# Expert weights split in place in ten to twelve homes, with the down chunks two blocks behind

## The reference

```python
def swiglu(h, w1, w3, w2):
    return (jax.nn.silu(h @ w1) * (h @ w3)) @ w2

def moe_swiglu(h, w_router, w1, w3, w2):
    logits = (h @ w_router).astype(jnp.float32)
    top_val, top_idx = lax.top_k(logits, TOP_K)
    top_w = jax.nn.softmax(top_val, axis=-1)
    combine = jnp.sum(jax.nn.one_hot(top_idx, N_EXPERTS, dtype=jnp.float32) * top_w[..., None], axis=-2)
    out = jnp.zeros_like(h)
    for e in range(N_EXPERTS):
        out = out + combine[..., e:e + 1].astype(h.dtype) * swiglu(h, w1[e], w3[e], w2[e])
    return out
```

## Time and profile before

| | |
|---|---|
| median of 3 runs | 1847.54 us (1846.96 to 1848.07) |
| the profiled execution, its own time | 1846.31 us |
| its span | 1844.6 us |
| TensorE clock granted in it, share of full | 0.998 |
| PE busy | 1795.8 us, 97% of the span |
| DVE busy | 1526.0 us, 83% |
| ACT busy | 1236.8 us, 67% |
| moved by DMA | 519.91 MB, mean 282 GB/s |

### The profile page before, as it was taken

The page is one execution under the profiler, slowest core; times in us unless marked ns, Lnnn a source line. Parts: engine busy times, 40 slices in busy tenths (PEclk is TensorE's granted clock), DMA queues, the critical chain, the costliest instruction groups (busy, mean ns, idle before and its releaser), DMA issues.

```text
span 1844.6 us, 25231 instructions
## 1 busy us (share of the span) xinstructions
PE 1795.8 (97%) x10094; PEld 1523.3 (83%) x10094; DVE 1526.0 (83%) x1402; ACT 1236.8 (67%) x1144; POOL 76.7 (4%) x97
## 2 busy tenths in 40 slices
PE   9999999999999999999999999999999999999997
PEld 9989998999999989998988766787677876778765
DVE  7999866575558999965598899888998899988997
ACT  5656745554445566744576788778887788877886
POOL 1000000100001000000200000000001000010000
PEclk9999999999999999999999999999999999999999
DMA  8544554445445544545399999999999999999994
GB/s 335 182 163 158 183 183 160 155 178 193 182 159 180 195 160 160 183 183 183 139 388 390 343 408 421 393 376 370 418 421 397 374 366 422 421 396 370 373 421 190
DMA packets 75845, 519.91 MB, mean 282 GB/s; under 512 B 9360, under 2 KB 9616, under 8 KB 14544
## 3 DMA queue, kind: packets, MB, share of 16 engines
q1 hardware_dynamic: 72464, 507.84, 71.3%
q0 software_dynamic: 2544, 9.18, 1.7%
q10 hardware_dynamic: 720, 1.31, 0.2%
HBM read 511.74 MB, written 6.55 MB: 281 GB/s over the span
## 4 chain that ended last, share of the span: by engine, by line
PE 74%; DVE 16%; ACT 6%; issue 3%; DMA 1%; SPq 0%; ACTq 0%; DVEq 0%
PE psum L1946 15%; PE psum L1932 13%; PE psum L1934 13%; PE psum L1933 13%; DVE wlo L1205 13%; PE psum L1947 7%; ACT whi L665 5%; PE psum L2434 3%; PE psum L2435 2%; PE psum L2453 1%; DVE U L1789 1%; PE psum L2200 1%; PE psum L2180 1%; DMA raw<-in_stream 1%; PE psum L2416 1%
## 5 line engine op out<-in xcount | busy, mean ns | idle before, releaser
L1205 DVE TENSOR_TENSOR wlo<-raw,whi 128x2048 fp32r<-128x2048 f32 x369 | 837.3, 2281 | 194.0 <-ACT whi L665 192.8
L665 ACT ACTIVATE whi<-raw 128x2048 fp32r<-128x2048 f32 x369 | 700.0, 1904 | 144.9 <-PE psum L1934 82.2
L1946 PE MATMUL psum<-h_hl,whi 128*128 128x512 f32 x1216 | 430.1, 398 | 0.3 <-DVE U L1563 0.2
L1947 PE MATMUL psum<-h_hl,wlo 128*128 128x256 f32 x1216 | 340.3, 280 | 0.0
L1932 PE MATMUL psum<-whi,act_hl 128*128 128x512 f32 x736 | 293.3, 399 | 7.9 <-DVE wlo L1205 6.4
L1934 PE MATMUL psum<-whi,act_hl 128*128 128x512 f32 x736 | 287.7, 391 | 0.0
L1933 PE MATMUL psum<-wlo,act_hl 128*128 128x512 f32 x736 | 287.3, 390 | 0.0
L1946 PEld LDWEIGHTS psum<-h_hl,whi 128*128 128x128 f32 x1216 | 228.2, 188 | 55.0 <-issue 1.2
L1947 PEld LDWEIGHTS psum<-h_hl,wlo 128*128 128x128 f32 x1216 | 229.5, 189 | 0.1
L1932 PE MATMUL psum<-act_hl,whi 128*128 128x256 f32 x720 | 206.3, 287 | 1.4 <-DVE wlo L1205 0.7
L2434 PE MATMUL psum<-whi,h_hl 128*128 128x512 f32 x448 | 183.7, 410 | 21.0 <-DVE wlo L1205 20.3
(11 more groups left out here) (295 smaller groups left out, 2231.7 us busy)
## 6 DMA issues: line engine op xcount, KB each, us to landing
raw<-in_stream SPq DMA_DIRECT2D x366, 1024.0 KB, 6.7
U<-in_stream SPq DMA_DIRECT2D x74, 1024.0 KB, 8.2
memhat<-in_stream SPq DMA_DIRECT2D x37, 1024.0 KB, 8.0
raw<-in_stream SPq DMA_DIRECT2D x6, 512.0 KB, 3.8
xacc<-U POOLq DMA_DIRECT2D x3, 512.0 KB, 7.6
xT<-in_x_cols ACTq DMA_DIRECT2D x4, 256.0 KB, 6.5
raw<-in_stream SPq DMA_DIRECT2D x4, 256.0 KB, 7.2
memhat<-in_mem_cols SPq DMA_DIRECT2D x1, 1024.0 KB, 19.7
```

The source lines that it names most:

```text
L665: act.activation(whi[:, n % SPLIT, 0:words], src[:, 0:words], ACT.Copy).then_inc(hi_ready, 1)
L1205: dve.tensor_tensor(wlo[:, n % SPLIT, 0:words], src[:, 0:words], whi[:, n % SPLIT, 0:words].bitcast(F32), ALU.subtract).then_inc(lo_ready, 1)
L1946: pe.matmul(o[:].rearrange("p (a b) -> p a b", a=2), st[0], mv, start=start, stop=False)
L1947: return pe.matmul(o[:, 0:256], st[1], mv[:, 0, :], start=False, stop=stop)
```

## The change

In the expert part the low part is written into the home itself, over the raw words, so that `wlo` isn't used there; a home is free only when PE has used the chunk. There are ten homes (a part of `h_hl` is the tenth) until chunk 46 (`JOINED`), and twelve from there on (`xT` and another piece of `U`). The high homes stay three. The down chunks of step s stand behind the ups of step s + 2 (they stood behind those of s + 1). In a few step the turn stands behind the ups (before: between gates and ups), and the fold behind the downs (before: between ups and downs). The gathered tokens of the next expert are transposed by halves in steps f = 4 and 5, through bank 7, behind the ups; only expert 0 still does all of it in step 6. `halves_kept`, `rows_out` and the routing's small work move by one or two chunks.

```diff
-EXTRAS = 3
+EXTRAS, LATER = 4, 2
 RING = RAW + EXTRAS
+DEPTH = SPLIT
+JOINED = 46
...
 def gate_end(s):
-    return 6 * s - 1 if s else 1
+    return 6 * s - 3 if s > 1 else 4 * s + 1
...
 def down_end(s):
-    return up_end(s + 1) + 2 if s < STEPS - 1 else TOTAL - 1
+    return min(up_end(s + 2) + 2, TOTAL - 1 - 2 * (STEPS - 1 - s))
...
+def due(n, end):
+
+    return next((s for s in range(STEPS) if end(s) + lead(s) == n), None)
...
+        def lo_home(n):
+
+            if MOE <= n < MOE + TOTAL:
+                return slots_r[SLOT_OF[n - MOE]]
+            return wlo[:, n % SPLIT, :]
...
-                if n >= RING:
-                    sp.wait_ge(lo_ready, MOE + n - RING + 1)
+                if BEFORE[n] is not None:
+                    sp.wait_ge(w_used, MOE + BEFORE[n] + 1)
...
+            def next_tokens(s):
+
+                p, f = divmod(s, FSTEPS)
+                if p == 0 and f == FSTEPS - 1:
+                    for k in range(2):
+                        gathered(2, 1, k, bank[gate_bank(s + 1) + k][:])
+                elif 0 < p < NE - 1 and f in (4, 5):
+                    gathered(p + 2, p + 1, f - 4, bank[7][:])
...
+                        if few_step(s):
+                            act.activation(gsum, bank[gate_bank(s)][:], ACT.Copy).then_inc(halves_out, 1)
+                        else:
                             if s > 1:
                                 act.wait_ge(e_g, s - 1)
                             act.activation(esil[:, s % 2, :], bank[gate_bank(s)][:], ACT.Silu).then_inc(e_silu, 1)
-                        if s:
-                            transposed(s, s - 1, few_step(s - 1))
...
+                            if s:
+                                transposed(s, s - 1, few_step(s - 1))
+                                next_tokens(s)
...
+                    p = ended(n, down_end, 2)
+                    if p is not None and few(p):
+                        halves_kept(p)
...
-                dve.tensor_tensor(wlo[:, n % SPLIT, 0:words], src[:, 0:words],
-                                  whi[:, n % SPLIT, 0:words].bitcast(F32), ALU.subtract).then_inc(lo_ready, 1)
+                dve.tensor_tensor(lo_home(n)[:, 0:words], src[:, 0:words], hi_home(n)[:, 0:words].bitcast(F32),
+                                  ALU.subtract).then_inc(lo_ready, 1)
...
-                    if s:
+                    if s and not few_step(s):
                         turned(s - 1)
...
+                    for half in range(2):
+                        gated_part(s, half, 1)
+                    if few_step(s):
+                        turned(s - 1)
+                    if 0 < p < NE - 1 and f in (4, 5):
+                        if f == 5:
+                            pe.wait_ge(he_lo_s, 2 * p + 3)
+                        brought(p + 1, f - 4, bank[7])
...
-                    if f == FSTEPS - 1 and not last:
-                        brought(p + 1, gate_bank(s + 1))
-                    for half in range(2):
-                        gated_part(s, half, 1)
-                    if few_step(s):
-                        folded_gate(s)
...
-                    if s:
-                        for half in range(2):
-                            down_part(s - 1, half)
...
+                    if s > 1:
+                        for half in range(2):
+                            down_part(s - 2, half)
+                    if few_step(s) and s < STEPS - 1:
+                        folded_gate(s)
```

More of the change, by code:

```diff
@@ L134, in chunk_of, with rotation @@
                 return s // FSTEPS, first(s % FSTEPS) + k
+def rotation():
+    ring, last, at, before = list(range(RING)), {}, [], []
+    for n in range(TOTAL):
+        if n == JOINED:
+            ring = list(range(RING, RING + LATER)) + ring
+        i = ring.pop(0)
+        ring.append(i)
+        at.append(i)
+        before.append(last.get(i))
+        last[i] = n
+    return at, before
+SLOT_OF, BEFORE = rotation()
 G_MIX, G_X, G_MEM, G_FFN, A_CB, A_LG, A_LB, C_CW = 0, 16, 32, 48, 64, 72, 80, 88
@@ L1003, in _, with gathered @@
             x_rows(0)
[L1005 to L1013, removed]
+            def gathered(count, p, k, got):
+                act.wait_ge((ga_half, ga_done)[k], count)
+                if few(p):
+                    act.activation(he_few[:, 4 * k:4 * k + 4, 0:HALF], got[:, 0:4 * HALF].rearrange("p (a b) -> p a b", a=4),
+                                   ACT.Copy).then_inc(he_hi_s, 1)
+                else:
+                    act.activation(he_hi[:, 512 * k:512 * k + 512], got, ACT.Copy).then_inc(he_hi_s, 1)
             def transposed(count, f, few_rows):
@@ L1046, in first_round @@
             def first_round():
-                gathered(1, 0)
+                for k in range(2):
+                    gathered(1, 0, k, bank[2 + k][:])
                 act.wait_ge(wts_s, 1)
@@ L1101, in second_round @@
                 act.wait_ge(x_back, 4)
-                act.activation(wselT[:, 0, :], last_sel.bitcast(F32), ACT.Copy).then_inc(wt_kept, 1)
-                act.wait_ge(wt_kept, 1)
-                gathered(NE + 1, 0)
+                act.activation(wselT[:, 0, :], last_sel.bitcast(F32), ACT.Copy).then_inc(wt_ready, 1)
+                act.wait_ge(wt_ready, 1)
+                for k in range(2):
+                    gathered(NE + 1, 0, k, bank[2 + k][:])
                 for i in range(4):
@@ L1125, in body @@
                                 act.wait_ge(w_used, n_e + PER_E - 4)
-                                gathered(e + NE + 2, 0)
+                                for k in range(2):
+                                    gathered(e + NE + 2, 0, k, bank[2 + k][:])
                             transposed(k_e + FSTEPS, FSTEPS - 1, False)
@@ L1936, in wt @@
             def wt(n, k, cols, at, width):
[L1938 removed]
+                return tuple(w[:, k * cols + at:k * cols + at + width] for w in (hi_home(n), lo_home(n)))
             def parts(hi, lo, k):
```

196 lines of the change are left out of this document (118 added, 78 removed).

## The result

The changed kernel takes 1901.82 us (median of 4 runs, 1899.66 to 1903.22) where the kernel before takes 1847.25 in the same comparison: ratio 1.0295, interval 1.0277 to 1.0313. The forecast, 1882 with a range to 1894, had the direction and fell short by some 20 us. The profiled execution of the changed kernel spans 1901.0 us, 56.4 more than before.

The account below looks back on a forecast made before the run. Few experts were taken to run at DVE's pace, full ones at PE's. 3 x (8.9 + 2.6) - 5.4 + 5.95 = +35.05 us on 1846.31 gave 1881.4, 1882.6 as a median; stated 1882, range 1865 to 1894.

Parts of the forecast that it names:

- The gathered pieces, +29.1: Steps f = 4 and 5 of full experts 2, 4, 6: PE idles for transposes, piece, copy and subtraction, six times 4.85 us.
- Other things in a full expert, -0.8 in all: Full expert without gathers: four few down chunks instead of two -1.8, halves and entry +1.2, rest +0.3; -0.8 booked.
- +1.2 for the halves: Full expert: PE idles 1.8 us behind the halves' copies, where they cost 0.78 before; with 0.2 at entry, +1.2.
- A few expert, +2.6: Few expert goes from 104.4 to 107.0 us: +1.8 for two full down pairs instead of one, +0.8 for fold and pieces.
- Homes and in-place subtraction, nothing: Expert part: twelve homes released by PE cost nothing; subtracting in place costs nothing, bounds 0 to 0.1 us a chunk.
- a rival about the ring of loaded homes: Few steps: loaded homes are the bound, three more remove the 0.58 us gap in 28 steps, giving 1831; chance 0.05.
- Start, -5.4: Expert 0 has one full down pair fewer, -5.46 us, and 0.1 lost.
- Last expert, +5.95: Last expert has one full down pair more, 5.46 us, and its last pairs stand behind each other at 0.5 more.
- The end, nothing: From the last down matmul to the program's end: forecast change 0 us.

Follow-up runs that it names:

- experiment 1: Changed kernel, but in full experts ACT's and DVE's gathered piece stands behind the step's two down chunks: 1859.85 us, ratio 1.0072 to the kernel before.
- experiment 2: Changed kernel, but in full experts the gathered piece stands between the copies of the two down chunks: 1874.61 us.
- experiment 3: Changed kernel, but in full experts PE makes the four transposes between gates and ups, ACT's and DVE's lists as changed: 1862.48 us.
- Experiment 5: Changed kernel with 36 more identity transposes on PE, results unused, behind the four real ones in full experts: 1888.76 us.
- experiment 6: On top of experiment 1, the copies of the halves stand one chunk later in ACT's list: 1857.33 us.
- experiment 8: On top of experiment 1, in few steps the fold stands between ups and downs again and its silu one copy earlier: 1858.33 us.
- experiment 4: Kernel before with only the homes changed: low part in place, ten to twelve homes, loads released by PE: 1847.63 us, ratio 1.0008.
- experiment 10: Kernel before, its order kept, with in-place low parts, ten to twelve homes, the gain's home moved, six high homes, small work one chunk later: 1809.3 us.
- experiment 7: On top of experiment 1, DVE's gather places worked out two chunks earlier and the final gain loaded into a home done with earlier: 1856.95 us.

## Why the prediction was wrong, by its steps

1. **The gathered pieces, +29.1: the mechanism right, a part of its price missed.** From the transposes' start to the matmul the forecast had 5.1 to 5.25 and the trace shows 5.06 (1478.74 - 1473.68), of which 4.60 are idle; experiments 1, 2 and 3 show the cause and its dose. The step of the sum that failed is the price 6 x 4.85: it ends at "PE bounds these steps, so nothing gives it back", with nothing for what the idle does to the clock, 1.4 to 2.1 more behind each, 10 us in all. Experiment 5 shows it apart. The Trainium skill's "TensorE: Matmul & The Clock Gate", section "HAM oscillation — how this bites in real kernels", warns of just this, idle gaps of PE between bursts that drop its clock; the trace agrees (0.50 behind 4.6 idle), and the forecast had left the rule out. The trace of before did show that the clock can fall in this kernel: it is 0.66 in 1009 to 1014, though behind 32 narrow matmuls and not behind an idle stretch (last section). No row of the forecast asked for it. Apart from the clock such a step takes 22.09, 5.3 more than a plain one of 16.8 where 4.85 was booked: the idle was 0.2 shorter than forecast, but the transposes and their place cost 0.6 (experiment 1). That is 0.9 in a full expert.
2. **Other things in a full expert, -0.8 in all, of which +1.2 for the halves: right.** Without its two steps with a piece a full expert is 0.5 shorter than before. PE's idle stretch behind the halves' copies is 1.56, forecast 1.8; experiment 6 gives back 1.8.
3. **A few expert, +2.6: right**, 2.4 measured. The split into 1.8 for the full pair and 0.8 for fold and pieces is half tested (experiment 8).
4. **Homes and in-place subtraction, nothing: right** (experiment 4). The forecast had read the repeated gap of 0.58 by a rule of the Trainium skill's "Perfetto Trace Analysis", section "Optimization Strategy" (consistent bubbles can mean too few buffers), as a rival about the ring of loaded homes. That rival fell. The rule did not, as far as the runs tell: with six high homes a few step takes 14.1 in experiment 10, where it took 14.9, so the gap looks like a lack of high homes (experiment 10 also placed the small work one chunk later).
5. **Start, -5.4: the term right, a wait missing, and much of the difference is no effect of the change.** The full down pair did go: from the first matmul of the expert part to the end of expert 0's third step the changed kernel takes 40.0, where it took 46.4: 6.4 less, forecast 5.4. What came on top is a wait for the first gather, 1.8 to 2.7 in the executions that have it (2.0 more in that step in experiment 1, 3.4 here with the low clock behind it), which the forecast didn't count: it never asked how long DVE's index work at chunk 33 had now to reach PE (experiment 7). The other 5.9 are the difference from experiment 1's execution: the expert part's first matmul comes 2.9 later, at a clock of 0.50 ahead of it, the sixth step takes 1.6 more and the seventh 1.4.
6. **Last expert, +5.95: right**, 6.2.
7. **The end, nothing: wrong, +1.6.** The load of the final gain, which the change puts behind PE's last use of its home, got no term of its own (experiment 7). The other executions with that wait end 11.5 to 13.2 us behind the last down matmul, so 1.6 is this execution's.

Together: 13.5 for full experts over the forecast (10 of it the clock), 6.6 at the start (5.9 of it between executions), 1.6 at the end, -0.7 and +0.3 for the rest, 21.3 of 21.35. Without the 5.9 the profiled execution would have taken some 1897, still outside the range (an estimate). The range failed because all its bounds were of terms that the sum had; what was missing were terms.

## What to carry to other kernels

In an engine that works its list in order, place a small instruction by what it waits for: if it waits for PE, it must stand behind the copies that PE needs next. Price an idle stretch of PE of several microseconds above its length, because of the clock behind it: 6.35 for 4.6 here. And when a change frees a buffer (here the low homes), ask first which wait it could end. The waits of the earlier trace rows, ACT's copy for PE, pointed at the high homes all along, and giving them the freed memory, with the small work moved by a chunk, won 37 us where more of the other homes won nothing.

## What the runs showed that was not expected

- An idle stretch of 4.6 us on PE is followed by some 3 to 4 us at 0.50 of the clock, six times out of six. With it filled by 36 transposes of 128x128 the clock stays at 1.00, six times out of six.
- Of a shorter one no run tells a rule. Behind the six of 1.64 to 1.66 in experiment 2 the clock stays. Behind the wait for the first gather it falls in four executions (1.76 in the changed kernel, 2.66, 2.34 and 2.68 in experiments 2, 3 and 8) and stays in three (1.96, 2.04 and 1.90 in experiments 1, 6 and 5). In experiment 1, to be read beside the rows of experiment 7:

```profile
1022.78 0.71 PE L2596 MATMUL psum<-ident,U 64*128 64x64 f32 x8 [1.96 <-DMA U<-hrow,gidx]
...
1023.75 0.40 PE L2045 MATMUL psum<-raw_alias,act_hl 128*128 128x512 f32 x1
```

- The clock also fell where PE was never idle. In the kernel before, 32 matmuls with a moving side of only ten columns stand in expert 0's sixth step; the matmuls behind them run slow, and the windows view has a clock of 0.66:

```profile
1005.18 3.64 PE L2367 MATMUL psum<-U 128*128 128x10 f32 x32
...
1010.36 0.63 PE L1934 MATMUL psum<-whi,act_hl 128*128 128x512 f32 x1
```

```profile
1009.00:1014.00 5.00, 5.00 (x16) 3.95 (x15) 1.80 (x6) 0.64 (x1) 1.16 (x2) 0.66 1.01 418
```

- The same instructions run at full clock in some executions and at half in others. The stretch from 912 to 919 is at 0.50 in the changed kernel and at 1.00 in experiment 1; expert 0's sixth step takes 22.0 in experiments 1, 5 and 6 and 23.6 in experiments 2, 3, 7, 8 and the changed kernel. The end of expert 0's last step lies at 1034.2 in experiment 1 and at 1041.0 in experiment 2, 6.8 us of difference between single profiles that no edit there made. One kernel's own runs show it too: the four of experiment 8 took 1855.89 and 1856.08 at a mean clock of 0.998 and 0.997, and 1860.58 and 1862.14 at 0.995. What decides it stays open.
- A subtraction of 128x2048 in place takes 2288 ns, as one into another buffer.
